# A two-layer decoder step on one core: the projection in four overlapped parts, sample rows as fp32 products in column groups

## The reference

```python
kv = rmsnorm(x, g_norm) @ w_kv          # (rows, 1024) @ (1024, 2048): keys, then values
qz = rmsnorm(x, g_norm) @ w_in          # (rows, 1024) @ (1024, 2048): queries, then gates
a = p[:, :, 0] - lam * p[:, :, 1]       # two softmaxes per head, their difference applied to v
y = (o.reshape(b, t, D_B) * jax.nn.silu(z)) @ w_out
```

## Time and profile before

| | us |
|---|---|
| median of 3 runs | 3381.88 (3379.08 to 3382.13) |
| profiled execution | 3381.49 |
| its span, first to last instruction | 3379.7 |
| PE busy | 3126.8 (93%) |
| PE weight loads busy | 2582.6 (76%) |
| DVE busy | 1581.0 (47%) |
| ACT busy | 1188.3 (35%) |
| DMA queue of SP | 429.59 MB, 40.0% of 16 engines' span |

### The profile page before, as it was taken

The page is one execution under the profiler, slowest core; times in us unless marked ns, Lnnn a source line. Parts: engine busy times, 40 slices in busy tenths (PEclk is TensorE's granted clock), DMA queues, the critical chain, the costliest instruction groups (busy, mean ns, idle before and its releaser), DMA issues. The chain is left out here.

```text
span 3379.7 us, 44652 instructions
## 1 busy us (share of the span) xinstructions
PE 3126.8 (93%) x17000; PEld 2582.6 (76%) x17000; DVE 1581.0 (47%) x2673; ACT 1188.3 (35%) x2149; POOL 95.8 (3%) x109
## 2 busy tenths in 40 slices
PE   5999999999978999799988999969999999787598
PEld 4888888889977888588876777749999999543486
DVE  4574655564641111331214312148888888332464
ACT  3333333342320000322113221137777777332222
POOL 0000000000000000000000000010000000000111
PEclk8999999999989999899998999979999999998799
DMA  4434343424233222343324423282445451686453
GB/s 138 137 106 137 106 137 106 139 100 170 83 106 98 90 93 86 120 144 127 128 101 138 138 102 116 93 185 54 111 103 112 103 110 30 263 309 234 168 177 115
DMA packets 249951, 431.96 MB, mean 128 GB/s; under 512 B 20889, under 2 KB 119961, under 8 KB 244217
## 3 DMA queue, kind: packets, MB, share of 16 engines
q1 hardware_dynamic: 249775, 429.59, 40.0%
HBM read 327.30 MB, written 102.95 MB: 127 GB/s over the span
## 5 line engine op out<-in xcount | busy, mean ns | idle before, releaser
L295 PE MATMUL proj_acc<-proj_w_hi,b_x_hi 128*128 128x512 f32 (+1 forms) x832 | 330.0, 397 | 0.0
L297 PE MATMUL proj_acc<-proj_w_hi,b_x_lo 128*128 128x512 f32 (+1 forms) x832 | 326.5, 392 | 0.0
L296 PE MATMUL proj_acc<-proj_w_lo,b_x_hi 128*128 128x512 f32 (+1 forms) x832 | 326.0, 392 | 0.0
L1290 ACT ACTIVATE attn_scores<-attn_scores,attn_lowest 128x1024 f32<-128x1024 f32 (+15 forms) x256 | 307.2, 1204 | 28.8 <-DVE attn_lowest L1343 28.8
L1230 PE MATMUL attn_s<-attn_k_hi_lo,attn_q_lo_hi 128*128 128x512 f32 (+3 forms) x640 | 266.3, 416 | 33.0 <-DMA attn_q_hi_lo<-qT_lo 28.6
L1260 PE MATMUL attn_o<-attn_v,attn_aT 128*128 128x128 f32 x2176 | 295.6, 276 | 1.0 <-ACT attn_aT L1301 1.0
L1260 PEld LDWEIGHTS attn_o<-attn_v,attn_aT 128*128 128x128 f32 x2176 | 279.4, 191 | 10.6 <-ACT attn_aT L1301 1.2
L1343 DVE CUSTOM_DVE_ANT_0 attn_scores<-attn_s,attn_bias 128x1024 f32<-128x1024 f32 (+7 forms) x256 | 216.7, 856 | 151.1 <-PE attn_s L1231 118.3
L295 PE MATMUL pool_acc<-pool_odd_x_hi,pool_wh 128*128 128x272 f32 (+1 forms) x768 | 249.1, 324 | 0.0
L296 PE MATMUL pool_acc<-pool_odd_x_lo,pool_wh 128*128 128x272 f32 (+1 forms) x768 | 248.5, 324 | 0.0
L297 PE MATMUL pool_acc<-pool_odd_x_hi,pool_wl 128*128 128x272 f32 (+1 forms) x768 | 248.3, 323 | 0.0
(11 more groups left out here) (223 smaller groups left out, 5833.8 us busy)
## 6 DMA issues: line engine op xcount, KB each, us to landing
pool_wu<-in_w_in_a SPq DMA_DIRECT2D x16, 2048.0 KB, 7.8
pool_wz<-in_w_in_a SPq DMA_DIRECT2D x16, 2048.0 KB, 7.7
smp_k_page<-in_cache_k SPq DMA_DIRECT2D x64, 512.0 KB, 5.4
smp_v_page<-in_cache_v SPq DMA_DIRECT2D x64, 512.0 KB, 5.6
pool_wm<-in_w_map_a SPq DMA_DIRECT2D x16, 1024.0 KB, 5.6
early_loads<-gatedT SPq DMA_DIRECT2D x16, 1024.0 KB, 5.9
proj_wst<-in_w_kv SPq DMA_DIRECT2D x8, 2048.0 KB, 9.4
proj_wst<-in_w_in_b SPq DMA_DIRECT2D x8, 2048.0 KB, 8.3
```

Source lines behind the costliest of these rows:

```text
L295: pe.matmul(out, ah, bh, start=first, stop=False)
L296: pe.matmul(out, ah, bl, start=False, stop=False)
L297: return pe.matmul(out, al, bh, start=False, stop=last)
L1290: act.activation(part, part, ACT.Exp, scale=-1.0, bias=low[s][:, x:x + 1], accum_out=sums[s][:, i:i + 1]).then_inc(expd, 1)
```

## The change

The two `project` calls become one object, `Project`, that goes through four parts of 512 rows (`parts`), each with the same eight units, now of four blocks. All 32 unit passes load and split their weights. A part's rows stand in one of two places in SBUF, and the next part's row blocks are normalised during the present part: block after block in units 1 to 4 (1 to 5 for the last part, which has the sample rows as a fifth block). Within such a unit SP loads the block one unit earlier, ACT squares at the first product and takes the root at the second, DVE averages and scales there, PE turns it after the third product, and high and low part follow at the fourth. `AHEAD` is 2 and only holds for part 0.

Of the three turning banks two serve the rows and one, `key_bank`, the keys; `turn_keys` waits for the low part of the key block just before. Two semaphores, one of ACT's and one of DVE's work, replace one for each slot.

The sample rows are a fifth step in each unit of the last part, and the first in its order. Their scaled rows are kept unsplit in `xs` (one copy for each gain), and they are multiplied in fp32 with the weights as loaded: for each of 8 slices, four products of 128 columns, each into its own 32 PSUM partitions. The result (128 x 128) is stored in four pieces.

The output layer loads blocks 2 and 3 of `gatedT` among its weight loads, and each later block two blocks sooner than before. The first weights and the first row block of the projection are loaded during it. In the last part, at unit 5, SP loads the first head's keys and one of the two query operands whole (4 MB); attention then awaits only two small pieces of the other query operand for its first pair, and four pieces for its second. Buffers are placed anew so that all this fits.

```diff
-        self.x_in = [m.sem(f"norm_x_in{i}") for i in range(ring)]
+        self.x_in = [first_in if i == 0 and first_in else m.sem(f"norm_x_in{i}") for i in range(ring)]
@@ OutLayer.run
                 self.load_w(sp, i)
+                if i in (3, 4):
+                    sp.wait_ge(g_lo, i - 2)
+                    load_g(sp, i - 1, i - 3, P)
...
+                if ahead:
+                    sp.wait_ge(g_lo, 2 * i + s + 3)
+                    load_g(sp, 2 * i + s + 4, s, ahead)
+                if x_n:
                     sp.wait_ge(out_sem[s], 16 * i + 16)
+                    load_x(2 * i + s + 2, s, x_n)
+            step(0, 0, P, P, P)
+            sp.wait_ge(w_lo, KC // LK)
+            nxt.load_w(sp, 0)
...
+            sp.dma_start(nxt.slots[0][:, :], D["x1"][0:P, :]).then_inc(nxt.row_sem, 16)
@@ Project.run
+        NS, NR = 5, 3
+        LATE = 2
+        self.turn_banks += [m.ps(f"turn{i}", [P, KC // 2, P]) for i in range(2)]
+        key_bank = m.ps("turn_keys", [P, CT, P])
+        order = [(CT, 0, 1, 2, 3) if first_block[p + 1] - first_block[p] > CT else (0, 1, 2, 3) for p in range(PN)]
+        steps = [(p, u, b) for p in range(PN) for u in range(NUN) for b in order[p]]
...
+        def norm_block(p, u):
+            if p + 1 == PN or not 1 <= u <= first_block[p + 2] - first_block[p + 1]:
+                return None
+            return first_block[p + 1] + u - 1
@@ sync
+            norm.load(sp, 1)
+            norm.load(sp, 2)
+            self.load_w(sp, 1)
+            norm.load(sp, 3)
+            for n, (p, u, b) in enumerate(steps):
+                w = p * NUN + u
+                if b == 0 and w >= 1 and w + 1 < NWU:
+                    sp.wait_ge(lo, w * KC)
+                    self.load_w(sp, w + 1)
+                if b == 0:
+                    c = norm_block(p, u + 1)
+                    if c is not None:
+                        norm.load(sp, c)
+                if p == PN - 1 and u == NUN // 2 + 1 and b == 0:
...
+                    nxt.first_loads(sp)
+                if transposed(n):
+                    store_turned(n)
+                else:
+                    store_rows(n)
+                late = late_keys(n)
+                if late is not None:
+                    store_turned(late)
@@ scalar (vector has the same order)
+            for n, (p, u, b) in enumerate(steps):
+                w = p * NUN + u
+                if b == 0 and w + 1 < NWU:
+                    split(w + 1)
+                if kind(n) == "z":
+                    r, a = take(act, n)
+                    act.activation(r, a, ACT.Silu).then_inc(taken_act, 1)
+                if transposed(n):
+                    turned_high(n)
+                late = late_keys(n)
+                if late is not None:
+                    turned_high(late)
+                c = norm_block(p, u)
+                if c is not None and b == 0:
+                    norm.square(act, c)
+                if c is not None and b == 1:
+                    norm.root(act, c)
+                if c is not None and b == 3:
+                    norm.high(act, c)
@@ tensor
+            def turn_keys(n):
+                i = k_index[n]
+                wait_taken(pe, n)
+                if i >= 1:
+                    pe.wait_ge(t_lo, t_index[by_k[i - 1]] + 1)
...
+            for n, (p, u, b) in enumerate(steps):
+                if b == 0:
+                    pe.wait_ge(lo, w * KC + KC)
...
+                for k in range(KC):
+                    if not whole(n):
+                        for j in range(CT):
+                            last = pe.matmul(a[j * R:(j + 1) * R, 0:P], xs[:, units[u][1][3], k, :],
+                                             wst[w % 2][:, k, j * P:(j + 1) * P], start=k == 0, stop=k == KC - 1)
...
+                late = late_keys(n)
+                if late is not None:
+                    turn_keys(late)
+                if n + AHEAD < first_block[1]:
+                    norm.turn(pe, n + AHEAD)
+                c = norm_block(p, u)
+                if c is not None and b == 2:
+                    norm.turn(pe, c)
@@ attention
-    FIRST_KQ = 160
+    FIRST_KQ = 64
...
+            for n in (4, 5):
+                load_kq(0, n, slice(near * P, (far + 1) * P), begin_in)
+            for n in (4, 5):
+                load_kq(0, n, slice(0, near * P), kq_in[0])
                 load_kq(0, n, slice((far + 1) * P, S), kq_in[0])
...
-                    pe.wait_ge(begin_in, 96)
+                    pe.wait_ge(head0.sem, 64)
+                    pe.wait_ge(begin_in, 32)
```

More of the change, by code:

```diff
@@ L172, with __init__ @@
 class Norm:
-    def __init__(self, m, blocks, ident, place, slots, junk, small, banks, gain, width):
+    def __init__(self, m, blocks, ident, place, slots, junk, small, banks, gain, width, first_in=None):
         self.blocks, self.ident, self.place, self.slots, self.junk = blocks, ident, place, slots, junk
@@ L842, in project @@
[L842 to L872, removed]
@@ new lines, in run @@
+        stores, last_k, plan, k_index, t_index = [0] * NS, [0] * NS, [], {}, {}
+        for n in range(len(steps)):
+            s = n % NS
+            by_act.append(by_act[-1] + (kind(n) == "z"))
+            by_dve.append(by_dve[-1] + (kind(n) != "z"))
+            plan.append((stores[s], last_k[s]))
+            if transposed(n):
+                t_index[n] = len(t_index)
+            else:
+                stores[s] += 1 if whole(n) else CT
+            late = late_keys(n)
+            if late is not None:
+                t_index[late] = len(t_index)
+            if kind(n) == "k" and whole(n):
+                k_index[n] = len(k_index)
+                last_k[s] = len(k_index)
@@ L880, in _, with store_turned @@
         @block.sync
         def _(sp):
[L882 to L890, removed]
+            def store_turned(n):
+                d = t_index[n]
+                p, u, b = steps[n]
+                i, name, t0 = units[u][0], kind(n), parts[p][0]
@@ L923, in _ @@
+            for s in range(NS):
                 sp.wait_ge(out_sem[s], 16 * stores[s])
@@ L962, in _ @@
[L962 to L973 removed]
+                act.activation(th[d % NR][:, :], source(n), ACT.Copy).then_inc(t_hi, 1)
@@ new lines, in _ @@
+            for n, (p, u, b) in enumerate(steps):
+                w = p * NUN + u
+                if b == 0 and w + 1 < NWU:
+                    split(w + 1)
+                if transposed(n):
+                    turned_low(n)
+                elif kind(n) != "z":
+                    copy_out(n)
+                late = late_keys(n)
+                if late is not None:
+                    turned_low(late)
+                c = norm_block(p, u)
+                if c is not None and b == 0:
+                    norm.average(dve, c)
+                if c is not None and b == 1:
+                    norm.apply(dve, c)
+                if c is not None and b == 3:
+                    norm.low(dve, c)
+                    if c == NBLK - 1:
+                        for i, bank, _, _ in norm.parts(c):
+                            ks = slice((i % 2) * KC // 2, (i % 2 + 1) * KC // 2)
+                            for g, gain in enumerate(gains):
+                                dve.tensor_tensor(xs[:, g, ks, :], bank, gain[:, ks].unsqueeze(2).broadcast_to([P, KC // 2, R]),
+                                                  ALU.mult).then_inc(xs_made, 1)
@@ L1070, in attention @@
+def attention(nc, D, K, S, H, head0, early, slot):
     NB = S // P
@@ L1995, in program @@
-        attention(nc, D, K, S, H)
+        gains = [K["gain_kv"], K["gain_b"]]
+        x1_blocks = [(D["x1"][b * P:(b + 1) * P, :], P) for b in range(S // P)] + [(D["x1"][S:NT, :], R)]
+        H = D["cache_k"].shape[2]
+        K["HD"] = D["lambda_q1"].shape[1]
+        size = 2 * KC * part
+        halves = lambda t: [t[:, i * KC * part:(i + 1) * KC * part].rearrange("p (k t) -> p k t", k=KC) for i in range(2)]
+        with ExitStack() as below:
+            even = Memory(nc, below, "even").sb("x", [P, size], F32R)
```

399 lines of the change are left out of this document (206 added, 193 removed).

## The result

| | before | after |
|---|---|---|
| median of 4 runs | 3381.89 (3379.08 to 3382.13) | 3405.00 (3404.78 to 3412.15) |
| ratio, 95% interval | 1 | 1.0075 (1.0058 to 1.0093) |
| span of the profiled execution | 3379.7 | 3403.3 |

The forecast was slower, 3420, with 3388 to 3450 as its range. So the direction and the mechanism held, and the size was +23.5 us (by the spans) in place of +38.6. 3405.0 lies on the lower edge of 3405 to 3435, which the prediction had called the forecast's own range.

What follows compares the result with a forecast made beforehand. PE was taken as the bound, busy 3126.8 of 3379.7 us. Costs of 45.0 + 40.4 + 19.8 less gains of 66.6 gave +38.6 on 3381.49: 3420 us, own range 3405 to 3435, 3388 to 3450 to 0.8.

Steps and rivals of the forecast that it cites:

- output layer: Output layer: third block already loaded, so PE restarts sooner and loses less to half clock; -7.1 us.
- start of the projection: Ahead of the first product: first row and weights already there, so ACT's split and every later step move earlier; -6.2 us.
- second start: PE's 28.5 us stop ahead of the second projection half goes, less turning four more blocks; -26.4 us (-30 to -24).
- sample rows: Projection: eight times 64 fp32 instructions at 0.06 us each replace eight 5.44 us products; -12.4 us (-28 to +12).
- start of attention: First query pair awaits only two small operand pieces and POOL's bias, and PE goes on at once; -14.5 us (-16 to -11).
- key bank: Both query units of parts 0 to 2: PE waits for the previous key's low part, six times 7.5 us; +45.0 us.
- row blocks: Projection units: PE waits for the next part's scaled rows, squared only behind the weight split; +40.4 us (25 to 55).
- clock: PE at half clock after nine stops of about 7 us, 2.2 us lost each; +19.8 us (0 to 25).
- The clock did not stay up: Answers the rival that PE's clock stays up over a stop of 7 us: 3400 us, chance 0.12.
- Crowding: Rival: weight loads twice as often beside the same stores land 1.5 us later, lengthening all 20 waits: 3450 us, chance 0.12.
- only the bank would stall: Rival: only the key bank waits come, since the row blocks fit in somehow: 3379 us, no change, chance 0.08.
- The faster side: Rival: splits early enough, so no waits come and only gains stay, given loads some 7 us earlier: 3315 us, chance 0.10.

## Why the prediction was right, and where its sizes were not

| step | predicted | measured | how |
|---|---|---|---|
| output layer | -7.1 | -9.1 | last product, 1365.6 for 1374.7 |
| start of the projection | -6.2 | -6.4 | gap of 20.0 for 26.4 |
| second start | -26.4 | -24.3 | 53.7 (805.0 less the 751.3 without stops) less the sample rows |
| sample rows | -12.4 | -29.4 | 8 x (5.56 - 1.89) |
| start of attention | -14.5 | -17.4 | all behind the projection |
| key bank | +45.0 | +45.2 | waits, six |
| row blocks | +40.4 | +34.9 | 80.1 idle less the key waits |
| clock | +19.8 | +29.7 | PE busy, 780.9 less 751.2 |
| sum | +38.6 | +23.2 | spans: +23.6 |

Measured and forecast terms differ in both directions: the clock cost 10 us more than forecast, and without that the sum would have missed by 25 us and not by 15. Two terms of the prediction are not quite what their own figures give, 7.2 for 7.1 in the output layer and 14.9 (2243.9 less 2229.0) for 14.5 in attention.

**The key bank** came as forecast: six places, none in the last part, each 6.8 to 8.1 us where 7.0 and 8.7 could be read in the earlier trace rows. The forecast of this term worked since the whole chain (load issued, weights landed, split, low part) stood in the trace of before, harmless, and only the position of PE's turn had to be moved on it. The last part's one key wait (3.3 us) is of another kind: in its right key unit PE waits for DVE's first copy, which is late behind the split. I had 2.8 us there for two.

**Row blocks**: z units 6.3, 5.7 and 7.2 for 6.9; v units 2.2, 2.6 and 2.2 for 3.1; the rest 8.7 for 11. A little less each time, from the same chain.

**The sample rows** are the term that was mis-sized, by 17 us, more than the whole difference of 15. I had read 0.06 us for each instruction from the sixteen of 4 columns in the earlier trace rows, which start within 0.95 us. The time line of the kernel before, without the filter by line that I had used, shows what else PE did there:

```profile
3091.46 0.59 PE L1703 MATMUL smp_o_ps<-smp_o_parts,smp_fold 128*32 128x512 f32 x1
3091.47 0.24 PE L1649 MATMUL smp_a_new<-smp_k_new_now,smp_q_diag 128*32 128x4 f32 x6
3091.89 0.59 PE L1703 MATMUL smp_o_ps<-smp_o_parts,smp_fold 128*32 128x512 f32 x1
3092.32 0.27 PE L1649 MATMUL smp_a_new<-smp_k_new_now,smp_q_diag 128*32 128x4 f32 x10
```

Two products of 512 columns stand among them: most of the 0.95 us was theirs, and the ten that follow undisturbed span 0.27 us, 0.027 each at most. So the 0.06 was no distance between starts. The other row of the group, 16 on 512 columns in 1.92 us, was the one to scale: 0.12 us each, a quarter of it for 128 columns is 0.030, and 64 of them are 1.92 us for the 1.89 measured. That was the lower bound, -28. Of the remaining 1.4, 1.0 is that a sample step had taken 5.56 us, not 5.44.

The Trainium skill (TensorE: Matmul & The Clock Gate, Back-to-back issue gap), which the prediction weighed, has a floor of about 25 ns between starts or, in another decode mode, 62. The step on half of the columns has 0.016 us between the records of its starts, under both; for products in four column groups this case does not bear that floor out.

**The clock** cost up to 2.3 us a stop (29.7 over 13, or 2.1 by the 28 us that the half-clock stretches account for) where I had 2.2. The count was off: I gave it to nine stops of about 7 us. It is granted at 0.50 in 13 stretches of the changed kernel's projection, 3.4 to 10.2 us long, three of them behind v-unit stops of 2.2 to 2.6 us and one behind the stop of 3.3. Over the experiments the loss follows the idle time: 80.1 idle with 29.7, 57.5 with 19.7, 28.4 with 12.5, none with none.

**Output layer and attention** gained 2 and 3 us more than forecast. The weight loads did not pay for the two blocks between them (I had charged 2 us), and PE stood for only 3.1 us before the third block, 3.4 us at half clock. In attention, 9.1 and 3.7 us of idle time stand where 16.4 and 12.4 did: the wait moved from the operands to POOL's bias, as forecast.

**The rivals.** The clock did not stay up. Crowding as a cost of all waits is out: the median landing of a weight load was 8.6 us (`w_in`) and 9.0 us (`w_kv`) where it was 8.3 and 9.5 before, and with early loads a DMA share of 0.53 did no harm. Only the one load beside the first head's operands was late. That only the bank would stall is out with 34.9 us of row blocks. The faster side was right in its condition: with a load issued a unit earlier, all waits vanish, 3301; it had put 3315, being short by the sample term.

## What to carry to other kernels

- When a unit of work is halved, write down for the new unit when each helper's result is ready and when it is wanted; what is long (here 10 us of landing and 5 us of split at the head of two queues) and was harmless in a unit of 44 us fills most of one of 22. Put prefetch work behind the work that the current unit waits for, or start its transfer earlier: either edit alone turned a loss of 0.75% into a gain of 2.5% (ratio 0.9750).
- A wait names the place where lateness shows, not its cause: doubling the bank named in the list moved half of it to the next wait.
- Before a duration for each instruction is taken from a filtered row, look at the same stretch unfiltered for products of other lines among them.

## What the hardware showed beyond what was expected

Three stops of 2.2 to 2.6 us in the changed kernel were followed by 3.4 us at PEclk 0.50 with PE busy throughout, which is some 1.7 us more for each. That does not always happen: in the kernel with the split one product later, stops of 2.4 and 3.0 us (1656.07 and 1850.49) were followed by none. Fp32 products of 32 output columns in four column groups stream side by side: 1.89 us for 64 instructions in four groups, 7.10 in one. And PE's product of 24 matmuls took 5.44 us in the first and third part and 5.56 in the second and fourth at the same granted clock of 1.00; the second half of the kernel before had 5.56 too. What differs is the place in SBUF that the rows are read from, but this wasn't tested, and the cause stays open.
